# A residual stage whose VectorE splits the next weight panels before, not after, the low half of its own result

## The reference

```python
h = h + swiglu_ffn(h, ffn_norm[layer], ffn_w_in[layer], ffn_w_out[layer])   # @ w_out: 2816 -> 1024
h = h + nsa_attention(h, ...)          # ends in @ w_out: 1024 -> 1024
x = x + memory_cross_attention(...)    # ends in @ w_o: 512 -> 1024
# each followed by rmsnorm(h, gain) @ w of the next sub-layer
```

## Time and profile before

| what | value |
|---|---|
| median of 3 runs | 2722.52 us (2721.83 to 2725.18) |
| the profiled execution | 2722.52 us, of which the span of instructions is 2720.7 us |
| mean granted TensorE clock | 0.980 |
| TensorE matmul busy | 2603.9 us (96%) |
| TensorE weight load busy | 2122.1 us (78%) |
| VectorE busy | 1430.1 us (53%) |
| ScalarE busy | 946.1 us (35%) |
| GpSimd busy | 372.8 us (14%) |

### The profile page before, as it was taken

The page is one execution under the profiler, slowest core; times in us unless marked ns, Lnnn a source line. Parts: engine busy times, 40 slices in busy tenths (PEclk is TensorE's granted clock), DMA queues, the critical chain, the costliest instruction groups (busy, mean ns, idle before and its releaser), DMA issues.

```text
span 2720.7 us, 34006 instructions
## 1 busy us (share of the span) xinstructions
PE 2603.9 (96%) x12132; PEld 2122.1 (78%) x12132; DVE 1430.1 (53%) x2139; ACT 946.1 (35%) x1659; POOL 372.8 (14%) x313
## 2 busy tenths in 40 slices
PE   6988999999999999999998898999999999999999
PEld 5866888877777788888777786788878877688887
DVE  5896444435787544443443565544434656544422
ACT  5454332223466323222333434332222124333221
POOL 2003000011166400012100040200011050300000
PEclk9999999999999999999998998999999998999999
DMA  4202333223200232322321022233323332133322
GB/s 147 78 1 62 94 99 93 81 97 128 82 1 1 63 100 93 98 79 93 115 72 32 16 95 60 80 98 95 92 86 107 95 95 93 55 100 93 96 97 70
DMA packets 61149, 219.82 MB, mean 81 GB/s; under 512 B 7152, under 2 KB 7408, under 8 KB 60672
## 3 DMA queue, kind: packets, MB, share of 16 engines
q1 hardware_dynamic: 58896, 209.15, 24.8%
q0 software_dynamic: 2160, 9.44, 1.0%
HBM read 216.47 MB, written 2.10 MB: 80 GB/s over the span
## 4 chain that ended last, share of the span: by engine, by line
PE 84%; DVE 10%; ACT 3%; issue 1%; POOL 1%; ACTq 0%; DMA 0%; DVEq 0%; SPq 0%; POOLq 0%
PE psum L212 24%; PE psum L214 24%; PE psum L213 24%; DVE conv_out L847 3%; DVE wl L195 2%; PE psum L1904 2%; PE psum L1881 1%; ACT wh L189 1%; PE psum L1210 1%; PE psum L1158 1%; DVE x L743 1%; PE psum L2713 1%; PE psum L2109 1%; PE psum L1864 1%; PE psum L1863 1%
## 5 line engine op out<-in xcount | busy, mean ns | idle before, releaser
L212 PE MATMUL psum<-xh,wh 128*128 128x512 f32 x1880 | 739.0, 393 | 32.1 <-DVE wl L195 23.5
L213 PE MATMUL psum<-xl,wh 128*128 128x512 f32 x1880 | 735.2, 391 | 0.0
L214 PE MATMUL psum<-xh,wl 128*128 128x512 f32 x1880 | 735.0, 391 | 0.0
L189 ACT ACTIVATE wh<-raw 128x1024 fp32r<-128x1024 f32 x404 | 421.6, 1057 | 783.3 <-PE psum L214 777.1
L195 DVE TENSOR_TENSOR wl<-raw,wh 128x1024 fp32r<-128x1024 f32 x404 | 551.7, 1378 | 145.6 <-ACT wh L189 143.0
L212 PEld LDWEIGHTS psum<-xh,wh 128*128 128x128 f32 x1880 | 354.4, 189 | 108.0 <-issue 24.0
L214 PEld LDWEIGHTS psum<-xh,wl 128*128 128x128 f32 x1880 | 354.1, 188 | 75.9 <-issue 0.8
L213 PEld LDWEIGHTS psum<-xl,wh 128*128 128x128 f32 x1880 | 354.6, 189 | 74.5 <-issue 0.6
L212 PE MATMUL psum<-hidden_high,wh 128*128 128x512 f32 x704 | 276.5, 393 | 4.3 <-DVE wl L195 3.8
L213 PE MATMUL psum<-hidden_low,wh 128*128 128x512 f32 x704 | 274.2, 390 | 0.0
L214 PE MATMUL psum<-hidden_high,wl 128*128 128x512 f32 x704 | 274.0, 389 | 0.0
(11 more groups left out here) (381 smaller groups left out, 3288.6 us busy)
## 6 DMA issues: line engine op xcount, KB each, us to landing
raw<-ffn_in SPq DMA_DIRECT2D x176, 512.0 KB, 3.5
raw<-ffn_out SPq DMA_DIRECT2D x64, 448.0 KB, 4.2
raw<-ffn_out SPq DMA_DIRECT2D x32, 512.0 KB, 3.6
raw<-pw SPq DMA_DIRECT2D x24, 512.0 KB, 3.5
raw<-o_w_hgg SPq DMA_DIRECT2D x12, 512.0 KB, 4.2
raw<-w_q SPq DMA_DIRECT2D x8, 512.0 KB, 3.6
raw<-w_o SPq DMA_DIRECT2D x8, 512.0 KB, 3.5
raw<-e_w_qk SPq DMA_DIRECT2D x8, 512.0 KB, 3.5
```

Of the source, the lines that this page charges most:

```text
L189: self.nc.scalar.activation(self.wh[:, slot, :], self.raw[:, slot, :], ACT.Copy).then_inc(self.weights_high.sem, 1)
L212: nc.tensor.matmul(out, ah, bh, start=start, stop=False)
L213: nc.tensor.matmul(out, ah, bl, start=False, stop=False)
L214: return nc.tensor.matmul(out, al, bh, start=False, stop=stop)
```

## The change

In VectorE's part of `Residual`, the splitting of the next panels (`split_low`, called through `ahead`) moves from behind `xl` to before it. No instruction is added or removed, and the other engines' programs stay as they are. VectorE's wait for `xh` moves with `xl`; its wait for `weights_high`, which is in `split_low`, now stands ahead of `xl`.

```diff
                 else:
                     dve.tensor_tensor(c.x[:, at, :], out, c.x[:, at, :], ALU.add).then_inc(c.banks_freed.sem, 1)
+                for j in self.panels_of(m):
+                    c.ahead(c.split_low, dve, self.panel0, j, i, self.body_panels)
                 if self.gain:
                     dve.wait_ge(self.high.sem, self.high0 + m + 1 + self.body * i)
                     dve.scalar_tensor_tensor(c.xl[:, at, :], c.x[:, at, :],
                                              c.col(self.gain[0], self.gain[1] + m + self.body * i),
                                              c.xh[:, at, :].bitcast(F32), ALU.mult, ALU.subtract).then_inc(
                         self.ready.sem, 1)
-                for j in self.panels_of(m):
-                    c.ahead(c.split_low, dve, self.panel0, j, i, self.body_panels)
```

## The result

The changed kernel takes 2748.16 us (median of 4 runs, 2745.88 to 2749.48) against 2722.18 us of the kernel before (4 runs, 2720.45 to 2725.18). The ratio is 1.0098, 95% interval 1.0083 to 1.0112: 26 us slower, where 17 were forecast. That is 0.16 us above the upper end of the range, 2748, which is less than these runs differ among themselves. Of 15 further runs of the same kernel 14 took 2745.10 to 2755.08 us, and one, at 2906.2 us with a mean granted clock of 0.864, is left out of every comparison. The profiled execution took 2749.61 us, with a span of 2747.8 us and a mean granted clock of 0.975 (before: 2720.7 us and 0.980), so the two spans are 27.1 us apart. In the changed kernel `xl` is line 748; the other lines named here keep their numbers.

A forecast was written before the change was run, and what follows sets the result against it. TensorE's matmuls fill 96% of the span, so VectorE's order counts only where TensorE waits. -6.9 (gain) + 9.6 (feed-forward ends) + 2.5 (1024-wide) + 7.4 (cross-attention) + 4.5 (clock) = +17.1 on 2722.52: 2739 us, range 2728 to 2748.

The forecast's parts named there:

- What holds `wl` back, and the gain: Inside feed-forward outputs: `wl` stands still for GpSimd's `ssq`; without `xl` in front both end 0.36 us earlier, gaining 6.9 us.
- no gain inside: Rival, inside feed-forward outputs: `ssq` isn't shortened, so `wl` takes over at the same time; +24 us, 2746; chance 0.10.
- Loss where a feed-forward output ends: The next stage's first product waits for the last `xl` behind three `wl`: 3.13, 3.07 and weighted 3.37, together 9.6 us.
- nothing measurable: Rival: cross-attention losses and part of the clock's vanish because what follows waits anyway; +5 us, 2728; chance 0.09.
- faster: Rival: the next stage's first product is already held up as late, hiding tail losses; only the gain remains, 2716; chance 0.05.
- The clock, at these ends: Behind three feed-forward ends, TensorE's idleness brings a slow clock: 1.5 us each, 4.5 in all, bounds 0 and 8.
- clock holds: Rival: the clock does not fall at the three feed-forward ends; +12.6 us, 2735; chance 0.20.
- I take 1.5 each, 4.5: Slow clock's price at three feed-forward ends, taken from earlier stretches of 13 and 6 slow full-width matmuls, 2.6 and 1.2 us.
- The cross-attention ends have their slow stretch already; 0 more: Two cross-attention ends: no added clock loss; their waits and slower pairs alone cost 3.7 us each, 7.4 together.
- near 4.4: Sign: at the cross-attention ends the next stage's 22nd matmul waits near 4.4 us for `xl`, 1.73 before.
- VectorE, idle 0.6 us before each `x`, has room for the 0.4 that the new order adds: Inside four 1024-wide outputs: no loss; only their ends cost, 0.85, 1.03 and twice 0.3, together 2.5 us.
- The bounds of 0 and 4 for the four stages: Range for the 1024-wide ends' 2.5 us loss; 4 if `xl` has to wait for `ssq` once more.

The follow-up runs named there:

- e1: Kernel before with the feed-forward loop written out straight, new order only in feed-forward products 0 to 6: 2711.89 us against 2721.01; measured again, 2712.72 against 2721.72.
- e0: Kernel before with VectorE's two-turn loop written out straight in the feed-forward outputs, old order kept: 2719.58 us against 2721.01, ratio 0.9999.
- e7: Kernel before, old order, with GpSimd's addition to `ssq` cut to 64 of its 512 columns: 2700.64 us against 2721.59, ratio 0.9933.
- e5: Changed kernel plus 13 unused matmuls before TensorE's wait for the 8th `xl` at the three feed-forward ends: 2738.13 us against 2721.59 for the kernel before.
- e2: Kernel before with the feed-forward loop written out straight, new order only in the last product of three feed-forward outputs: 2735.16 us against 2721.01, ratio 1.0053.
- e4: Kernel before with the new order only in the two cross-attention outputs: 2728.65 us against 2721.01, ratio 1.0029.
- e3: Kernel before with the new order only in the four 1024-wide outputs: 2729.71 us against 2721.59, ratio 1.0033.
- e6: Changed kernel with GpSimd's squares and sums of the memory replaced by constant writes: 2747.82 us against 2721.59 for the kernel before, ratio 1.0091.
- e9: Changed kernel with the old order in o_w_out alone: 2747.49 us against 2721.72 for the kernel before, ratio 1.0089.

## Why the prediction came out 9 us low

The waits were right, the price of the clock was not, and one stage went another way. Step by step:

- **What holds `wl` back, and the gain: right.** `ssq` 1.30 us, `wl` 0.36 earlier, -7.7 us for 6.9 (-6.0 in e1 against e0). e1 and e7 show the cause: with the order kept and `ssq` short, the wait goes too. The rival "no gain inside" fell, although its 2746 is nearer to the measured total than the forecast is: it would have been right by luck.
- **Loss where a feed-forward output ends: right.** With the clock kept up in e5, the loss was 3.14 and 3.03 us for 3.13 and 3.07. The weighted end wasn't isolated. The rival "nothing measurable", that what follows waits anyway, fell with e2; so did "faster".
- **The clock, at these ends: mis-sized.** That it falls was right, and the rival "clock holds" fell. "I take 1.5 each, 4.5" measured 6.29 - 3.13, 7.42 - 3.37 and 6.26 - 3.07, so 3.2, 4.1 and 3.2: 10.4 in all, above the stated bound of 8. It left out what is no full-width matmul: the first five of the eight `L385` sums took 1.06 us slow and 0.61 at full speed (the rows above end there), all eight 1.70 and 0.95. With these 0.75 us, 12 x 0.2 = 2.4 becomes the 3.15 that e5 gives at the first end. And 1.5 lies between the stretches of 6 and 13 slow matmuls (1.2 and 2.6 us), where there were 12, 12 and 13. That is 5.9 of the 9 us, the largest part.
- **"The cross-attention ends have their slow stretch already; 0 more": wrong by 2.** The waits were right (4.33 us for "near 4.4", "in" +1.20 for 1.25, and +1.19 with e4 alone). The stretches grew from 13 and 6 matmuls to 14 and 14; the second, of 1.2 us, became a full one. In all 9.5 for 7.4.
- **"VectorE, idle 0.6 us before each `x`, has room for the 0.4 that the new order adds": the step that failed.** It was taken for all four 1024-wide outputs. The idle time had been read at w_o (0.62 to 0.65 us there). At pw2, w_o and e_w_out the loss holds to 0.1 us; at o_w_out it doesn't. GpSimd comes out of the memory's squares four products late, and from then on VectorE and GpSimd take turns to the end of the stage, and `xl` behind `wl` costs 1.78 us, not 0.74. So `x` fell 2.4 us behind TensorE, the first product of the next stage waited 2.39 us for its last `xl`, and the clock fell for 3 us more. 5.7 us for 0.3. e3 (the new order there alone brings it), e6 (without the memory's squares it is gone) and e9 (with the old order it is gone) show it; that e_w_out escaped because the memory's work began earlier there is read from its trace, and no run shifted that work; e5, with a wait but no slow stretch there, parts the 5.7 into 2.7 and 3.0. The bounds of 0 and 4 for the four stages had no room for it.
- **The rest:** 2.4 us less in stretches that the change doesn't touch hid some of the error, by luck.

By these: 17.1 - 0.8 (gain) + 5.9 (clock) + 2.1 (cross-attention) + 5.4 (o_w_out) - 0.1 (the other 1024-wide ends) - 2.4 (elsewhere) = +27.2, against 27.1 between the spans.

Of the rule in the Trainium skill (SBUF — State Buffer, Who interferes with whom), the lock is borne out, also by e7 and by the turns in o_w_out. Taken word for word, "for the whole instruction", it would have given 3.1 us more of gain than my rows. The trace doesn't agree: the 7.7 us measured (6.0 in e1) lie within 0.9 of the 6.9 by rows, and 2.3 or more from the 10.0 by the rule.

What stays open is what decides the length of a slow stretch. Behind the cross-attention's waits of 0.95 and 1.73 us 6 to 14 full-width matmuls were slow in the kernels with the old order there, and behind 2.38 us at o_w_out of e5 none. The Trainium skill (TensorE: Matmul & The Clock Gate, What's actually happening) says that the number of slow matmuls at a start differs between runs of one kernel. It speaks of a kernel's start; behind the waits here the traces agree, with 13 and 10 at the two cross-attention ends of e1 and 11 and 13 at those of its second profile.

## What to carry to other kernels

A reordering on an engine that is half idle is decided at the ends of stages: ask for each stage which result the next one needs, and in which product it is last, and change the order only where that isn't it. In the feed-forward outputs the same swap gains 6 us in products 0 to 6 and loses 17 at product 7, by the distances of e1 and e2 against e0 (8 and 16 by the totals). Price a wait of TensorE of two microseconds or more as the wait and 3 us of slow clock behind it, and consider cheap matmuls into a free bank to bridge it. Check "has room" in every stage that shares the code, with what the other engines do at that time; and measure parts by local distances too, since totals differ by 3 to 5 us from where slow stretches happen to fall, even between runs of one kernel (2734.86 to 2746.56 us in e5).

## What the runs showed of the hardware

- VectorE and GpSimd, with instructions that each read two tiles of on-chip memory, held each other up: `ssq` took 1.30 us, 1.66 behind `xl`, and the three `wl` behind it 4.45 us, 3.50 with a short `ssq` (e7). In o_w_out of the changed kernel, with neither engine pausing, they took turns: each instruction ended 0.5 to 1.2 us after the other's, and took 1.5 to 2.2 us where it takes 0.7 to 1.3 undisturbed.
- One TensorE wait of 2.0 to 3.8 us behind long full-speed work was followed by 10 to 14 slow full-width matmuls at 13 of the 15 ends of stages that had one, by 7 at one (e2) and by none at one (e5). At the three ends where e5 had none, it had cost 3.0 to 3.2 us in the changed kernel. With the wait filled by unused matmuls, none followed at four of five ends (at the fifth 0.87 us of idle time was left, and 6 matmuls were slow), and the real ones came no later.
- Writing out VectorE's loop of two turns straight gave TensorE 1.2 to 1.4 us inside each of three feed-forward outputs, without any other change (e0); the total stayed the same, and why is not shown.
